# Layer two of a hybrid decoder step: who adds the weighted values of the cached samples, and in how many parts the weight sums are made

## The reference, cut to what matters

```python
def _dilated_decode(q, kbuf, vbuf, kn, vn, d, nk):
    ...
    s = jnp.einsum('bthd,btmhd->bhtm', q, kg).astype(jnp.float32) * (q.shape[-1] ** -0.5)
    pr, lse = _masked_softmax_stats(s, valid[None, None])
    o = jnp.einsum('bhtm,btmhd->bthd', pr.astype(vg.dtype), vg)
    return o, lse.transpose(0, 2, 1)
...
wts = jax.nn.softmax(jnp.stack(lses, axis=0), axis=0)
ydil = jnp.einsum('gbth,gbthd->bthd', wts, jnp.stack(outs, axis=0).astype(jnp.float32))
```

## Time and profile before

| | |
|---|---|
| median of 3 runs | 1785.59 us (1785.54 to 1785.86) |
| profiled execution, its own time | 1785.21 us |
| its span, first to last instruction | 1783.4 us |
| PE busy | 1752.8 us, 98% of the span |
| DVE busy | 850.1 us, 48% |
| ACT busy | 620.0 us, 35% |
| POOL busy | 460.0 us, 26% |
| granted clock of TensorE | 1.00 (mean of the span) |
| chain that ended last | PE 88%, DVE 6%, ACT 3%, DMA 1%, issue 1% |

### The profile page before, as it was taken

The page is one execution under the profiler, slowest core; times in us unless marked ns, Lnnn a source line. Parts: engine busy times, 40 slices in busy tenths (PEclk is TensorE's granted clock), DMA queues, the critical chain, the costliest instruction groups (busy, mean ns, idle before and its releaser), DMA issues.

```text
span 1783.4 us, 22466 instructions
## 1 busy us (share of the span) xinstructions
PE 1752.8 (98%) x8302; PEld 1372.6 (77%) x8302; DVE 850.1 (48%) x1792; ACT 620.0 (35%) x1504; POOL 460.0 (26%) x511
## 2 busy tenths in 40 slices
PE   8999999999999999999999999999999999999998
PEld 4577765888888888747558888888888888779573
DVE  0444422785666556451332543354435444776613
ACT  1411234654565244311311133423332333843311
POOL 0151100335222012400003552254326443223000
PEclk9999999999999999999999999999999999999999
DMA  8311111245655245541121012223132434844412
GB/s 270 133 60 66 65 44 43 60 159 168 204 168 164 83 98 152 186 144 48 56 74 49 27 46 87 74 67 106 43 113 72 142 114 133 273 144 148 155 69 96
DMA packets 148807, 196.21 MB, mean 110 GB/s; under 512 B 19068, under 2 KB 107900, under 8 KB 148563
## 3 DMA queue, kind: packets, MB, share of 16 engines
q1 hardware_dynamic: 140580, 174.65, 31.1%
q10 hardware_dynamic: 8118, 20.14, 3.0%
HBM read 156.97 MB, written 37.85 MB: 109 GB/s over the span
## 4 chain that ended last, share of the span: by engine, by line
PE 88%; DVE 6%; ACT 3%; DMA 1%; issue 1%; POOL 0%; SPq 0%; ACTq 0%; DVEq 0%
PE PS L3173 48%; PE PS L2208 11%; PE PS L2252 4%; PE PS L375 3%; PE PS L1995 3%; PE PS L539 3%; PE PS L287 2%; PE PS L2031 2%; PE PS L2006 2%; PE PS L2028 1%; DVE WK L708 1%; PE PS L901 1%; PE PS L894 1%; PE PS L1315 1%; PE PS L2220 1%
## 5 line engine op out<-in xcount | busy, mean ns | idle before, releaser
L3173 PE MATMUL PS<-HT,RING 128*128 128x258 f32 (+2 forms) x1776 | 444.4, 381 | 2.6 <-ACT WK L3263 2.1
L3173 PEld LDWEIGHTS PS<-HT,RING 128*128 128x128 f32 x1776 | 329.1, 190 | 48.8 <-ACT WK L3263 2.9
L3263 ACT ACTIVATE BIG<-PS 128x256 f32<-128x256 f32 (+2 forms) x140 | 53.7, 383 | 355.4 <-PE PS L3173 355.0
L3173 PE MATMUL PS<-BIG,RING 128*128 128x258 f32 (+1 forms) x656 | 159.8, 382 | 1.3 <-DVE BIG L3359 1.3
L2208 PE MATMUL PS<-BIG 128*128 128x512 f32 x328 | 147.7, 597 | 0.5 <-DVE BIG L3370 0.5
L3173 PEld LDWEIGHTS PS<-BIG,RING 128*128 128x128 f32 x656 | 122.9, 190 | 19.9 <-DVE BIG L3359 2.1
L2208 PEld LDWEIGHTS PS<-BIG 128*128 128x128 f32 x328 | 60.3, 190 | 69.8 <-issue 68.7
L3173 PE MATMUL PS<-BIG,WK 128*128 128x258 f32 (+1 forms) x448 | 112.4, 382 | 1.0 <-DVE BIG L3359 1.0
L3173 PE MATMUL PS<-HT,CST 128*128 128x256 f32 (+2 forms) x432 | 110.4, 382 | 1.4 <-DVE BIG L3364 1.3
L3173 PEld LDWEIGHTS PS<-BIG,WK 128*128 128x128 f32 x448 | 83.3, 190 | 13.4 <-DVE BIG L3359 1.4
L3173 PEld LDWEIGHTS PS<-HT,CST 128*128 128x128 f32 x432 | 79.4, 190 | 13.4 <-DVE BIG L3364 3.0
(11 more groups left out here) (398 smaller groups left out, 3117.9 us busy)
## 6 DMA issues: line engine op xcount, KB each, us to landing
RING<-in_w_in_a SPq DMA_DIRECT2D x14, 1024.0 KB, 6.1
WK<-in_cache_mem_kv SPq DMA_DIRECT2D x56, 256.0 KB, 5.6
RING<-in_w_kv_b SPq DMA_DIRECT2D x12, 1024.0 KB, 5.3
RING<-in_w_in_b SPq DMA_DIRECT2D x12, 1024.0 KB, 5.5
WK<-in_cache_win SPq DMA_DIRECT2D x40, 256.0 KB, 4.8
RING<-in_w_mkv SPq DMA_DIRECT2D x16, 512.0 KB, 5.1
BIG<-in_x_prompt SPq DMA_DIRECT2D x16, 512.0 KB, 3.3
BIG<-sample_query SPq DMA_DIRECT2D x28, 256.0 KB, 6.0
```

Of the source, the lines that this page charges most:

```text
L3173: last = nc.tensor.matmul(PS[:, bank, 0:mid - lo], weight_block(u // 2, s, k), h_block(layer_of(u), u % 2, t, k), start=(k == 0 and j not ...
L3263: nc.scalar.activation(part(u, n2 if j == 0 else n1, lo, mid), PS[:, banks(u)[0], 0:mid - lo], ACT.Copy).then_inc(sig("projections_copied" ...
```

## The change

The two additions of a cached sample of layer two (set "D") go from DVE to POOL. DVE keeps the product of the first tile and signals it (`first_tile_weighted`). POOL waits for ACT's two scaled tiles and for that signal, adds tile 1, waits for its own addition, and adds tile 2. PE waits for the semaphore values that the new counting gives (`weighted`). `sum_pair` becomes a generator, `sum_parts`, of three parts (`S3` and a21+a22; `S2`; `S4`), which layer two advances by one part per slot, in slots 8, 9 and 10 of 14; the additions of a sample stand between them in POOL's program. The semaphore `memory_turned` of the kernel's start is given up and its count folded into `turned_for_act`.

```diff
@@ sample_values_dve, and new functions after it
+            if name == "D":
+                last.then_inc(sig("first_tile_weighted").up(), 1)
+                return
             for t in range(1, nt):
                 last.then_inc(step.up(), 1)
                 dve.wait_ge(step.sem, step.n)
-                if name == "D" and t == 1:
-                    dve.wait_ge(*scaled_by_act("value", b))
                 last = nc.vector.tensor_tensor(v[0], v[0], v[t], ALU.add)
             last.then_inc(sig("values_weighted").up(), 1)
+
+        def weighted(name, b):
+
+            return sig("values_weighted").sem, {"A": b + 1, "D": NS + 2 * (b + 1), "B": 3 * NS + b + 1}[name]
+
+        def sample_values_pool(pool, b):
+
+            v = value_tiles("D", b)
+            pool.wait_ge(*scaled_by_act("value", b))
+            pool.wait_ge(sig("first_tile_weighted").sem, b + 1)
+            if b == 0:
+                pool.wait_ge(sig("values_weighted").sem, NS)
+            nc.gpsimd.tensor_tensor(v[0], v[0], v[1], ALU.add).then_inc(sig("values_weighted").up(), 1)
+            pool.wait_ge(sig("values_weighted").sem, NS + 2 * b + 1)
+            nc.gpsimd.tensor_tensor(v[0], v[0], v[2], ALU.add).then_inc(sig("values_weighted").up(), 1)
...
-            pe.wait_ge(sig("values_weighted").sem, NS * SMP[name]["order"] + b + 1)
+            pe.wait_ge(*weighted(name, b))
...
@@ sum_pair
+            for _ in sum_parts(pool, p):
+                pass
+
+        def sum_parts(pool, p):
...
             then(last, 5)
+            yield
...
             then(last, 6)
+            yield
...
@@ layer_b_pool
                 for p in scaled_pair_at(x - 1):
-                    sum_pair(pool, p)
+                    parts = sum_parts(pool, p)
+                next(parts, None)
+                for b in values_at(x - 1):
+                    sample_values_pool(pool, b)
```

More of the change, by code:

```diff
@@ L301, in build @@
         NORMS = "0AB"
+        MEMORY_TURNS = 4
         def squares_added(x, n):
@@ L364, in stage0_pe @@
                 if ft % 2 == 1:
-                    last.then_inc(sig("memory_turned").up(), 1)
+                    last.then_inc(sig("turned_for_act").up(), 1)
             def memory_products(l, kt):
@@ L407, in stage0_act @@
             for b in range(4):
-                act.wait_ge(sig("memory_turned").sem, b + 1)
+                act.wait_ge(sig("turned_for_act").sem, b + 1)
                 nc.scalar.activation(MEMT.rearrange("p (b x) n -> p b (x n)", b=4)[:, b], PS[:, b, :],
@@ L905, in stage2_act @@
         def stage2_act(act):
-            act.wait_ge(sig("turned_for_act").sem, 1)
+            act.wait_ge(sig("turned_for_act").sem, MEMORY_TURNS + 1)
             nc.scalar.activation(FLOOR.rearrange("p c h -> p (c h)"), PS[:, 6, 0:NU],
@@ L1016, in state_copy_act @@
         def state_copy_act(act, h):
-            act.wait_ge(sig("turned_for_act").sem, h + 2)
+            act.wait_ge(sig("turned_for_act").sem, MEMORY_TURNS + h + 2)
             nc.scalar.activation(CO[:, h, :], PS[:, state_bank(h), :], ACT.Copy).then_inc(sig("c_copied").up(), 1)
@@ L3045, in layer_b_pool @@
             sum_pair(pool, PA + 1)
+            parts = iter(())
             for x in range(SLOTS):
```

## The result

| | before | after |
|---|---|---|
| median of 6 runs | 1785.53 us (1784.58 to 1785.86) | 1792.61 us (1791.96 to 1795.56) |
| profiled execution | 1785.21 us, span 1783.4 | 1791.96 us, span 1790.2 |
| granted clock, mean of the span | 1.000 | 0.998 |

The ratio is 1.0045 (95%: 1.0035 to 1.0055). The change makes the kernel 7.1 us slower. The forecast was 1792.0 us, in a range of 1788.0 to 1796.5. The time is right, and so is its largest term. The mean clock, 0.998, is recorded for the other executions of after too (0.997 in the slowest), while those of before beside the experiments have 0.999 or 1.000, save one. So what lowers it isn't a matter of the profiled execution alone.

A forecast was written before the change was run, and what follows sets the result against it. The prediction took PE, at work for 98% of the span, to bound the kernel. It summed 1785.21 + 2.3 + 3.7 + 0.4 = 1791.6, plus 0.4 for the median: 1792.0 us, range 1788.0 to 1796.5.

The forecast's parts named there:

- What bounds the kernel, and the ceiling of 3.0 us: PE works 98% of the span; between 1512 and 1600 us a free DVE could give back at most 3.0 us.
- The wait that moves onto sample 5: Sample 5's first POOL addition now stands behind `S2` and the wait for six merged blocks: +3.7 us (3.0 to 4.1).
- What POOL's additions do to DVE: Both engines take turns reading SBUF, holding up DVE's merge: PE 2.3 us later by sample 4 (0 to 4.6).
- Behind that: From sample 5 to sample 6 PE takes 0.4 us more (0 to 1.0); sample 7 loses nothing.
- The fallen clock: Rival: clock falls in PE's new gap before sample 5, slowing the work behind: +1.7 to 3.5 us, about 1794.5; chance 0.30.
- The sum: 1785.21 + 2.3 + 3.7 + 0.4 = 1791.6, and 0.4 for the median of the runs: 1792.0 us.
- Taking turns costs nothing here: Rival: POOL's additions fall beside DVE's PSUM instructions and gaps, only the order counts: 1788.9 us; chance 0.16.
- The three parts elsewhere: In twelve pairs `S4` stands behind a move, with 2.4 to 3.8 us left before PE needs it: cost nothing.
- Not slower: Rival: relieved DVE finishes block 5's merge before PE reaches sample 5, and its waits vanish: 1782.6 us; chance 0.07.
- `S4` late: Rival: moves end over 2.4 us later, so `S4` stops PE in twelve pairs; 1 us each gives 1804; chance 0.03.

The follow-up runs named there:

- e3: Changed kernel plus ten matmuls that nobody reads on PE, right before its wait for sample 5; 1790.70 us, ratio 1.0032.
- e1: Changed kernel with the wait for six merged blocks back on `S4`, behind sample 5's additions; 1789.35 us, ratio 1.0026.
- e5: Changed kernel with sample 5's additions ahead of `S2` and of both waits for merged blocks; 1789.30 us, ratio 1.0020.
- e8: e5 plus matmuls that nobody reads on PE, three ahead of sample 1 and three ahead of sample 5; 1789.14 us, ratio 1.0023.
- e9: e1 plus matmuls that nobody reads on PE, three ahead of sample 1 and six ahead of sample 5; 1790.10 us, ratio 1.0026.
- e6: Kernel before with weight sums in three parts, plus sixteen POOL additions that nobody reads; DVE keeps its own additions; 1800.97 us, ratio 1.0082.
- e2: Kernel before with only the weight sums in three parts, the additions of the values left on DVE; 1785.95 us, ratio 1.0004.

## Why the prediction was right, and where only its sum was

**What bounds the kernel, and the ceiling of 3.0 us: right.** The three waits on DVE did vanish, and the work of PE behind each was caught by the next wait on POOL.

**The wait that moves onto sample 5: right, chain and size.** (The idle time adds up to 1.39 plus 3.0 to 4.1, so 4.4 to 5.5; the prediction has 4.5 to 5.6.) Predicted +3.7 us between samples 4 and 5, measured +3.65 and, in e3, +3.66; predicted 4.5 to 5.6 us of idle time, measured 5.04. `S2` did meet the merge (2.91 us instead of 2.31). e1 and e5 take the chain apart: 1.9 us go with the wait for six blocks, and with `S2` out of the way as well 1.92 of the 5.04 us are left.

**What POOL's additions do to DVE: the mechanism right, the term too large.** Predicted 2.3 us by sample 4, as the middle of 0 and 4.6; measured 1.04 in after, and 1.06 to 1.54 in e1, e3, e8 and e9, which have the same order there. The merge lost 24.2 - 18.2 = 6.0 us to the turns, but three of its eight blocks ran at 2.31 us beside no addition, and only the first three, 3.7 us of the loss, stand ahead of sample 4. The term also made DVE the engine that falls behind. The trace says otherwise: PE's three waits ahead of sample 4, 3.0 us, all end on POOL's second addition, in place of 1.6 us of waits for DVE's sums. The step that failed is the middle between two distant bounds. What could have been counted from the order and the times of before is how many additions fall on a merge, rather than on a PSUM instruction or an idle DVE. That the turns exist rests on e6; how the 1.04 us part between them and the 1.3 us longer path to each sample wasn't separated. For PE's 1.72 us before sample 1 the timelines give a reading: that sample's first tile came 0.56 us late behind the slow small instructions, and POOL's first addition started 0.15 us after the tile was ready, so the other 1.2 us are the longer path. But that is a reading, not an experiment.

**Behind that (+0.4): right in e3 (+0.13), wrong in after (+1.83).** The forecast's sum kept the clock at 1.00. The fallen clock was a rival with a chance of 0.30, priced at 1.7 to 3.5 us. The measured 1792.61 us lies in the range of either, so the time alone doesn't tell them apart; the granted clock does. The rival is what happened, at the low end of its price: 1.70 us in after, and 2.7 in e1 (8.81 us from sample 5 to 6 against e9's 6.12), where more of the slow time lay on work. What I held against it, that the first matmuls of the program ran at 1.00 after 6.6 us of idle time, said nothing about an idle time in the middle.

**The sum.** Predicted 2.3 + 3.7 + 0.4 = 6.4 us; measured in the profiled execution 1.04 + 3.65 + 1.83 - 0.17 = 6.35, plus 0.4 ahead of the stretch. The total is right by luck: a term 1.3 us too large stands beside a fallen clock of 1.7 us left out. Each of the two was within the range. Where the sum adds 0.4 us for the median over the profiled execution, 0.65 was measured. The 1788.9 us of the rival "Taking turns costs nothing here" don't follow from its terms: with the first at 0, the low ends give 1785.6 + 3.0 = 1788.6 and the chosen values 1789.7.

**The three parts elsewhere (nothing): right**, by e2 and by the slot matmuls' waits of after. **"Not slower": didn't occur**; the merge stayed behind L3389, as the argument against it said. **"`S4` late": didn't occur** in after; e6 shows what it looks like when it does, 2.5 us in one wait.

Open: why the clock falls behind one wait and not behind an equal one in another run; what part the turns have in the first 1.04 us; what parts e1's two groups; and the 1.9 us by which e9's median stands higher over before (4.6) than its stretch (2.74).

## What to carry to other kernels

Count an operation that moves to another engine as two changes: what the new engine has queued ahead of it, its old waits among that (here 3.65 of 6.35 us), and what the new pairing does to instructions that were undisturbed. When a change opens an idle gap on PE, put the work behind the gap at the low clock as well; filling the gap with matmuls that nobody reads (e3) tells how much of a loss that is. Compare two traces by intervals between fixed points of PE's work; totals of single executions hid both cancelling errors here.

## What was not expected of the hardware

- The granted clock fell behind short gaps of PE: some 2 us into the 5.04 us gap of after, behind a wait of 3.15 us in e1, of 2.2 us near 120 us in e9, and of 1.71 us in e5, there 0.3 us after PE had started again. The same 1.72 us wait in after left it at 1.00, and at the end of before it fell only 4.0 us after PE's last matmul. Behind these gaps it stayed at half for 3.41 or 6.83 us. The Trainium skill, "TensorE: Matmul & The Clock Gate", Part 1, says that the throttled clock is the default and activity lifts it; the trace agrees: in after the clock fell while PE was idle and came back while it worked.
- Where DVE's merge and POOL's additions met, DVE paid: 4.43 us in after and up to 5.80 in e6 (at 1585.16) for eight instructions that take 2.31, while POOL's additions in after stayed at 1.26 to 1.32 us, next to 1.28 alone. In e6, beside DVE's own additions, POOL's pairs stretched as well, to 3.02 us from 2.6.
